# First mixer's first column group: tiles in pairs from the meta tile on, each tile's transposes one tile ahead; two weight pieces, two transposes and one set of squares in another place

## The reference

```
h = concat(meta, x)
h = h + gla_mixer(rms_norm(h, gla_norm))     # w_in: q, k (4 heads x 128), v, z (4 x 256), gate (16)
h = h + gdn_mixer(rms_norm(h, gdn_norm))     # w_in: q, k (8 heads x 128), v, z (8 x 256), beta, a
out = rms_norm(h, final_norm)[16:]
```

## Time and profile before

| | |
|---|---|
| three runs | 1458.61, 1459.02, 1460.88 us, median 1459.02 |
| the profiled execution | 1460.51 us, its span 1458.7 us |
| PE busy, share of the span | 1424.4 us, 98% |
| DVE, ACT, POOL busy | 757.4, 465.4, 413.3 us |
| granted TensorE clock, mean | 0.995 of full speed |
| SP waiting at L328 (`store_meta`) for DVE L723 | 16.1 us, once |

### The profile page before, as it was taken

The page is one execution under the profiler, slowest core; times in us unless marked ns, Lnnn a source line. Parts: engine busy times, 40 slices in busy tenths (PEclk is TensorE's granted clock), DMA queues, the critical chain, the costliest instruction groups (busy, mean ns, idle before and its releaser), DMA issues.

```text
span 1458.7 us, 21386 instructions
## 1 busy us (share of the span) xinstructions
PE 1424.4 (98%) x8458; PEld 1197.6 (82%) x8458; DVE 757.4 (52%) x937; ACT 465.4 (32%) x957; POOL 413.3 (28%) x359
## 2 busy tenths in 40 slices
PE   7999999999999999999999999999989999999997
PEld 5777799978888888999999999978866777777776
DVE  5223622234444346645545698789944654444442
ACT  5332731133222243333344633421232632111121
POOL 3212043442101122121221177244342441222210
PEclk9999999999999999999999999999999999999999
DMA  6521244476444224544454322335368895555530
GB/s 200 162 84 40 87 129 149 146 255 201 164 159 166 77 61 114 134 102 116 124 153 146 89 83 67 100 93 170 116 219 231 244 230 150 150 142 159 166 87 29
DMA packets 213918, 200.35 MB, mean 137 GB/s; under 512 B 62873, under 2 KB 177065, under 8 KB 213570
## 3 DMA queue, kind: packets, MB, share of 16 engines
q1 hardware_dynamic: 207234, 187.53, 43.2%
q10 hardware_dynamic: 6592, 11.54, 2.9%
HBM read 131.93 MB, written 67.09 MB: 136 GB/s over the span
## 4 chain that ended last, share of the span: by engine, by line
PE 53%; DVE 6%; ACT 2%; DMA 2%; SPq 1%; issue 1%; DVEq 0%; POOLq 0%; ACTq 0%; POOL 0%
PE banks L2158 17%; PE banks L2970 12%; PE banks L2235 12%; DVE gdn L2488 4%; PE banks L2053 2%; PE banks L3059 2%; PE banks L3026 2%; PE banks L3031 2%; PE banks L2077 1%; DMA gdn<-gdn_v 1%; PE banks L3040 1%; PE banks L3014 1%; DMA gdn_z<-gdn 1%; PE banks L2983 1%; ACT gdn L2291 1%
## 5 line engine op out<-in xcount | busy, mean ns | idle before, releaser
L2158 PE MATMUL banks<-hn_hi,gdn 128*128 128x352 f32 x1488 | 309.8, 327 | 0.0
L2158 PEld LDWEIGHTS banks<-hn_hi,gdn 128*128 128x128 f32 x1488 | 244.5, 188 | 4.4 <-issue 2.7
L880 PE MATMUL banks<-gdn,hn_hi 128*128 128x512 f32 x528 | 168.0, 400 | 4.1 <-POOL gdn L602 3.1
L2158 PE MATMUL banks<-hn_lo,gdn 128*128 128x352 f32 x744 | 168.1, 321 | 0.0
L2235 PE MATMUL banks<-gdn,hn_hi 128*128 128x512 f32 x512 | 164.4, 401 | 1.8 <-ACT gdn L2434 1.4
L2488 DVE SCALAR_TENSOR_TENSOR gdn<-gdn,conv_taps,gdn 128x1040 f32<-128x1040 f32 x96 | 161.7, 1684 | 7.7 <-ACT gdn L2299 4.9
L2439 POOL TENSOR_TENSOR gdn<-gdn,gdn 128x1024 fp32r<-128x1024 f32 x31 | 84.1, 2713 | 270.9 <-ACT gdn L2274 270.9
L2158 PEld LDWEIGHTS banks<-hn_lo,gdn 128*128 128x128 f32 x744 | 127.2, 188 | 0.0
L880 PEld LDWEIGHTS banks<-gdn,hn_hi 128*128 128x128 f32 x528 | 99.2, 190 | 28.8 <-ACT gdn L432 3.9
L2235 PEld LDWEIGHTS banks<-gdn,hn_hi 128*128 128x128 f32 x512 | 96.2, 190 | 28.0 <-issue 3.1
L880 PE MATMUL banks<-gdn,hn_lo 128*128 128x512 f32 x264 | 104.2, 395 | 0.0
(11 more groups left out here) (316 smaller groups left out, 2299.3 us busy)
## 6 DMA issues: line engine op xcount, KB each, us to landing
gdn<-in_gdn_w_in SPq DMA_DIRECT2D x32, 512.0 KB, 4.1
gdn<-in_x SPq DMA_DIRECT2D x16, 512.0 KB, 3.7
gdn<-in_gla_w_in SPq DMA_DIRECT2D x32, 256.0 KB, 4.9
gdn_kq<-gdn SPq DMA_DIRECT2D x16, 512.0 KB, 3.8
gdn_v<-gdn SPq DMA_DIRECT2D x16, 512.0 KB, 3.4
gdn<-in_gdn_w_in SPq DMA_DIRECT2D x32, 256.0 KB, 4.5
gdn<-gdn_kq SPq DMA_DIRECT2D x16, 512.0 KB, 3.6
gdn<-gdn_ek SPq DMA_DIRECT2D x16, 512.0 KB, 5.8
```

Of the source, the lines that this page charges most:

```text
L880: mm = pe.matmul(out_bank(g, u, i), h_[:, kt, k], piece_of(w_, q), start=(kt == 0 and e == 0), stop=(kt == KT - 1 and e == 2))
L2158: return pe.matmul(acc[n % 2][:, b, 0:m], w[n % 2][:, kt, :], x[:, kt, PAD + s:PAD + s + m], start=(kt == 0 and e == 0), stop=(kt == KT - ...
```

## The change

Five edits:

1. In group 0 the tiles are taken as [0, 1], [2, 3], [4, 5], [6, 7], [8] (`UNITS_0`, read through `tiles(g, u)`, also by the evictions and stores). PE's program is `first_group`: tiles 0 and 1 take turns every two kt; `transposes(2)` stands before the last two kt of that pair; behind it every tile's 24 matmuls are done by themselves, with the transposes of the next tile in front of them. The product of the high part waits for `ai_hi` alone, the one of the low part for `ai_lo`.
2. In group 1, SP loads the last two pieces of group 2 ahead of `store_meta(1)`.
3. In tile 3 of the second mixer both transposes of k of head 0 stand behind kt = 7.
4. `squares(0)` stands behind `copy(2)` and `split_hi(4)` on ACT.
5. ACT's wait for `gd_cleared` is followed by a Copy of one column into `junk`, and POOL clears another slice of `junk`.

```
-    UNITS = [[0]] + [[t, t + 1] for t in range(1, NT, 2)]
+    UNITS = [None] + [[t, t + 1] for t in range(1, NT, 2)]
+    UNITS_0 = [[t, t + 1] for t in range(0, NT - 1, 2)] + [[NT - 1]]
...
+                    if 0 < g < NG - 2 and u == LAST - 1:
+                        load_piece(KT * (g + 1) + NST)
+                        load_piece(KT * (g + 1) + NST + 1)
                     if g and u == LAST - 1:
                         store_meta(g)
...
-                if g + 1 < NG - 1:
-                    load_piece(KT * (g + 1) + NST)
-                    load_piece(KT * (g + 1) + NST + 1)
-                else:
+                if g == 0:
+                    load_piece(KT + NST)
+                    load_piece(KT + NST + 1)
+                elif g == NG - 2:
...
+            def first_tile(t, i, u, kts):
+
+                for kt in kts:
+                    pe.wait_ge(S("ai_whi"), kt + 1)
+                    lo_ready(pe, kt)
+                    k = slice(t * P, (t + 1) * P)
+                    for e, (h_, w_) in enumerate(((T.hn_hi, hi), (T.hn_hi, lo), (T.hn_lo, hi))):
+                        if kt == 0 and e == 0:
+                            pe.wait_ge(S("ai_hi"), 2 * t + 2)
+                        if kt == 0 and e == 2:
+                            pe.wait_ge(S("ai_lo"), 2 * t + 2)
+                        mm = pe.matmul(out_bank(0, u, i), h_[:, kt, k], piece_of(w_, kt),
+                                       start=(kt == 0 and e == 0), stop=(kt == KT - 1 and e == 2))
+                    if kt == KT - 1:
+                        mm.then_inc(S("ai_mm"), 1)
+                    elif t == NT - 1:
+                        mm.then_inc(S("ai_wused"), 1)
+
+            def first_group():
+
+                for kt in range(0, KT, 2):
+                    if kt == KT - 2:
+                        transposes(2)
+                    for i, t in enumerate(tiles(0, 0)):
+                        first_tile(t, i, 0, range(kt, kt + 2))
+                for u in range(1, LAST + 1):
+                    for i, t in enumerate(tiles(0, u)):
+                        if t + 1 < NT:
+                            transposes(t + 1)
+                        if i == 0:
+                            free_banks(0, u)
+                        first_tile(t, i, u, range(KT))
...
-                if h is not None and kt >= 6:
-                    tr_k(h, kt - 6)
+                if h is not None and (kt >= 6 if h else kt == 7):
+                    for b in (kt - 6,) if h else (0, 1):
+                        tr_k(h, b)
...
+                if n == 3:
+                    squares(0)
...
-                h = 0 if n == 2 else head_of_q(n - 1) or None
+                h = head_of_q(n - 1) or None
...
+            act.wait_ge(E("gd_cleared"), 1)
+            act.activation(junk[:, 0, 0:1], T.minus_half[:, 0:1], ACT.Copy)
...
-            pool.memset(junk[:, 0, :], 0.0).then_inc(E("gd_cleared"), 1)
+            pool.memset(junk[:, 1, :], 0.0).then_inc(E("gd_cleared"), 1)
```

More of the change, by code:

```diff
@@ L225, in stored, with tiles @@
                 eng.wait_ge(S(f"ai_out{o % 4}"), 16 * (o // 4))
+        def tiles(g, u):
+            return UNITS[u] if g else UNITS_0[u]
         def place(g, u):
@@ L355, in sync @@
                 load_x(t)
-            store(0, 0)
+            for t in tiles(0, 0):
+                store(0, t)
             for t in range(6, NT):
@@ L362, in sync @@
                     if g or u:
-                        for t in UNITS[u]:
+                        for t in tiles(g, u):
                             store(g, t)
+                    if 0 < g < NG - 2 and u == LAST - 1:
+                        load_piece(KT * (g + 1) + NST)
+                        load_piece(KT * (g + 1) + NST + 1)
                     if g and u == LAST - 1:
@@ L371, in sync @@
                         store_pads()
-                if g + 1 < NG - 1:
-                    load_piece(KT * (g + 1) + NST)
-                    load_piece(KT * (g + 1) + NST + 1)
-                else:
+                if g == 0:
+                    load_piece(KT + NST)
+                    load_piece(KT + NST + 1)
+                elif g == NG - 2:
                     for n in range(3):
                         load_tile(n)
-                for t in UNITS[LAST]:
+                for t in tiles(g, LAST):
                     store(g, t)
@@ L442, in evict @@
             def evict(g, u):
-                for i, t in enumerate(UNITS[u]):
+                for i, t in enumerate(tiles(g, u)):
                     o = nth_out(g, t)
@@ L854, in free_banks @@
                     g_, u_ = (g, u - 2) if u - 2 >= FIRST[g] else (g - 1, u - 2 + LAST)
-                    pe.wait_ge(S("ai_ev"), nth_out(g_, UNITS[u_][-1]) + 1)
+                    pe.wait_ge(S("ai_ev"), nth_out(g_, tiles(g_, u_)[-1]) + 1)
             def meta_tokens(g):
@@ L875, in unit @@
                     for i, t in enumerate(UNITS[u]):
-                        if g == 0 and kt == 0:
-                            pe.wait_ge(S("ai_lo"), 2 * t + 2)
                         k = slice(t * P, (t + 1) * P)
@@ L957, in tensor @@
             transposes(1)
-            for u in range(len(UNITS)):
-                unit(0, u)
-                for t in (2 * u + 2, 2 * u + 3):
-                    if t < NT:
-                        transposes(t)
+            first_group()
             gate_low()
@@ L3352, in _ @@
         def _(act):
-            act.wait_ge(E("gd_cleared"), 1)
             F.scalar(act)
```

## The result

| | before | after |
|---|---|---|
| median of six executions each, same job | 1459.15 us (1458.25 to 1460.90) | 1447.70 us (1446.66 to 1450.41) |
| ratio, 95% interval | | 0.9918 (0.9907 to 0.9930) |
| profiled execution, span, mean clock | 1460.51, 1458.7 us, 0.995 | 1450.41, 1448.5 us, 0.996 |

The kernel is 11.5 us faster in the medians; the forecast was 9.8 us, to 1449.2 us, with 1446.4 to 1452.5 as the range. The two profiled executions differ by 10.1 us. PE's busy time is almost what it was (1.2 us less than in the earlier trace rows); what went is mostly idle time, and some time at half clock, in which PE counts as busy.

What follows compares the result with a forecast made beforehand. PE was taken as the bound, busy 1424.4 of 1458.7 us. Terms 5.4 + 2.3 + 2.1 = 9.8 us off the median of 1459.02 gave 1449.2 us, range 1446.4 to 1452.5.

Steps and rivals of the forecast that it cites:

- First group: Group 0's new tile order and transposes a tile ahead: PE's gaps and slow clock go, 5.4 us gained.
- the sign: First gate matmul, at the first group's end, expected at 72.3 us (71.5 to 73); forecast wrong if after 74.
- the prediction's own line: PE in group 0 without standing: 15.77 + 210 x 0.233 + 7 x 1.07 = 72.2 us at the first gate matmul.
- tightest place: Tile 2's transposes in group 0: rows ready at 22.63 us, PE wants them at 22.8, 0.1 us slack.
- second way of the sum: Group 0's gain from four PE gaps (3.8 us), slow clock and set costs: 5.1 to 5.3 us.
- case A: Part given back: tile 2's rows late with slow clock, or another stall becomes the next; 1451 to 1455 us, chance 0.16.
- Pieces 22 and 23: Start of group 2: earlier loads remove PE's stall at kt = 6, 2.3 us gained (0 to 2.4).
- Squares and transposes: Second mixer: earlier copy, taps and silu remove PE's wait at k's transposes; 2.1 us gained (0 to 3.0).
- The rest: The one-column Copy at the second mixer's start and the other cleared slice of `junk`: no effect.
- B: Group 0: each tile stopped by the next one's rows, needing an 8.8 us chain; above 1462 us, chance 0.02.
- C: PE's earlier start swallowed, for instance by a DMA chain at its own speed; 1457 to 1460 us, chance 0.03.
- D: Later waits shrink too, as tiles are evicted and stored earlier; 1444 to 1447 us, chance 0.06.

## Why the prediction was right, and where its sizes were off

*First group: 5.4 forecast, 6.35 between the two traces.* PE never stood, tile 2's transposes came at 23.54 (22.8 forecast), and the first gate matmul at 71.42, against 72.2 forecast and just outside the 71.5 to 73 given as the sign. Two sizes were off and partly cancelled, which is luck. A set of transposes was taken as 1.07 us; it is 6.44 - 24 x 0.233 = 0.85, so 7 x 0.22 = 1.5 us less. The prediction had spread the restart behind a pair over single sets, and thought that breaking up pairs costs 0.2 to 0.3 us. The trace of the kernel before and the variant without the tile ahead show the reverse: the restart was the low part's wait, and transposing a tile ahead removes it. Against that the slow pace ended later, which cost 16.53 - 15.77 = 0.76 us. With both put in, the prediction's own line gives 16.53 + 210 x 0.233 + 7 x 0.85 = 71.4.

At the tightest place, the rows of tile 2, the slack was therefore not 0.1 us but 0.8 (rows ready at 22.78). With the start filled PE comes there at 21.83 and still doesn't wait: the rows come earlier too, at 21.64. The second way of the sum, 5.1 to 5.3 us from the brackets, is too low because a bracket is less than what a wait costs between starts. Before tile 8's third product it is 0.87, while 67.24 - 65.42 = 1.82 us stand where two products take 0.47, so 1.35. The four waits come to about 1 us more in this way.

The Trainium skill, TensorE: Matmul & The Clock Gate (Part 1: The HAM clock gate), has the number of slow matmuls at a start differ from run to run. The traces agree: the slow pace ends at about 15.07 and at 18.02 in two traces of the kernel before, some three and nine matmuls, and at 16.53 and 16.08 in two of the changed kernel, six and five.

The prediction's case A drew on that for the 1.3 us of slow clock at 25.8 us. That stretch is not at the start, and it is the runs that show it missing in some executions, two traces of five. Where it is missing, the gate matmul stands at 76.0, and the group's gain is 4.7 us. The 0.95 us for the pieces, a term of the same sum, is missing in three of the five.

*Pieces 22 and 23: 2.3 forecast, 2.3 in the traces.* PE's shift grows from 6.3 us at the first logits behind group 1 to 9.0 us in the second mixer (531.39 to 522.39), and 2.3 of these 2.7 are this stall, which is gone. Alone 3.5 us (1.6 to 5.4).

*Squares and transposes: 2.1 forecast, 2.3 measured.* PE gets on behind DVE's copy 2.3 us earlier and its wait stayed at 0.62, within the 0.6 to 0.9 forecast. The three taps took 6.01 us, with POOL's split beside them as before. The prediction let the set of two edits bring the gain; the squares do it all.

*The rest.* The one-column Copy ran in an idle time of ACT. Sum forecast 9.8; the traces show 11.3 at 542 us and 10.2 at the end, the medians 11.5 and, in the later job, 12.4. The difference has two sources. The sets were 1.5 us cheaper, of which the slow start took back 0.8. And all three edits remove idle time of PE, behind which the clock sometimes fell; the prediction counted that once, at 25 us, as if it were in each execution. The mean clock of the 60 executions of the kernel before in the three later jobs is 0.9952, of twelve of the kernel after 0.9976. In the 60, those at 0.994 take 1461.6 us (nine) and those at 0.997 1458.8 us (twelve), 0.9 us for 0.001. By that some 2.2 us of the difference are clock. At 0.997 the two kernels take 1458.8 and 1448.6 us (two executions), 10.2 us apart, at 0.996 1459.8 (fourteen) and 1450.5 (two), 9.3 us apart, on both sides of the forecast sum. This is an estimate: the clock is known to three digits, and few executions of the kernel after lie at these values.

*The rivals.* B (a chain of 8.8 us a tile) and C (no change): nothing of them. But C's counterargument, that PE waits for no transfer in the body of the kernel, was too strong: the some 4 us at the start of the scan are waits for ACT, and ACT waits for stores. A's second half showed at the scan: in the first trace 1.1 us were given back there, by a longer stretch of half clock. Of the twelve executions after, three lie in D's 1444 to 1447 (1446.40, 1446.47, 1446.66), without a further wait having gone: it is the same kernel at a mean clock of 0.998 and 0.999.

## What to carry to other kernels

Transposing one tile ahead is worth more than the waits in PE's own list say: look at the weight loads for waits of a few tenths that repeat in every unit, and read a wait's cost from the starts of the rows on both sides of it. Where idle time goes, half clock may go with it, in some executions; count that as a chance and compare with several traces, not with one. Filling waits with matmuls that nobody needs brought no gain that six to twelve executions could show, at the start or at the scan.

## What the runs showed of the hardware

The granted clock shows 1.00 in every window of the first 20 us of the changed kernel, while its products take some 0.43 us each until 16.5 us and 0.23 later: the record alone doesn't tell the slow start. Filling 1.47 and 1.56 us of idle time before 12.2 us brought the fast pace from 16.5 to 12.7 us.

Behind the same waits of PE (some 1.08 and 0.91 us) the half clock came in three of five traces; behind the wait of 1.9 to 2.3 us at pieces 22 and 23 in two of eight; behind the one of 2.1 us for the silu in one of seven; behind 4 to 7 us of waits at the start of the scan in all twelve traces without fillings there, from 1.7 to 5.1 us of clock, and in one of the two with them.
